# A routed expert layer: the down product of 64-row blocks with high and low rows side by side

## The chip, the cores and the metric

The kernel runs on one core of a Trainium2 chip. The metric is the device time of one execution in microseconds. All operands are float32; a product of two such matrices is made from rounded "high" parts and remainders, "low" parts, so that one float32 product costs three products on TensorE (high by high, low by high, high by low).

## The reference, cut to what matters

The layer has a mixing part (convolution, pooling, projections), a mixture of experts and a gated per-token embedding. The change touches only the mixture of experts. Each of 1024 tokens goes to 8 of 64 experts, and an expert is a SwiGLU product:

```python
def expert_block(acc, blk):
    tok, g, e = blk
    xb = xt[tok]
    hb = jax.nn.silu(xb @ w_e_gate[e]) * (xb @ w_e_up[e])
    yb = (hb @ w_e_down[e]) * g[:, None].astype(xb.dtype)
    return acc.at[tok].add(yb), None
```

D is 1024 and the hidden width FF is 256, so `hb` is 256 wide and `yb` 1024 wide. The last product, `hb @ w_e_down[e]`, is the down product.

## The kernel before, in words

The mixing part and the router take the first 770 us or so. A table in SBUF then lists the tokens of each block. The first block of an expert has up to 128 rows; further blocks, where an expert has more tokens, have up to 64 (LESS). With these inputs there are 64 first blocks, 33 further ones, and no expert has more than one further block. After them comes a closing part (embedding, gate product, final norm).

The expert stage is one loop, `Fori(0, E // 2)`, with two experts in its body (`s` is 0 or 1), written separately for each engine, with semaphores between them. Each engine first reads the plan of its expert into registers (`plan_of`, line 558: a load and then an operation and an assertion for each value): `b` the block's number, `more` the number of blocks, `behind` how many further blocks came before, `ahead` the block to gather next. `wait_at` (lines 61 to 66) is a semaphore wait on a computed value followed by an increment of a gate semaphore.

TensorE, for expert e: transposes the next expert's gathered rows (`flip_rows`, line 1086, 8 transposes), runs the first half of the gate and up product (`up`, lines 1109 to 1114), transposes the hidden rows of the block before (`flip_hidden`, line 1104), runs the second half, transposes the 64 rows of the further block if there is one (`flip_less`, line 1091), and then makes the down product of the block before, `down(b, 1 - s)` (lines 1126 to 1140, 12 products of 128x512). The down product therefore lags one block. With a further block there follow `flip_hidden`, `up_less` (lines 1097 and 1098, 16 products, with the high and low rows of 64 tokens side by side as 128 columns of weights) and a second `down`, that of the expert's own first block. So the down product of a further block is the first one of the next expert's turn, and `down` has three waits ahead of its first product (`dn_split`, `h_rounded`, `y_read`) and one, `h_split`, after four.

ScalarE rounds to the high parts: the transposed rows (`round_rows`, line 1428), two pieces of down weights (line 1461), the hidden rows (`round_hidden`, line 1444), four pieces of gate and up weights (line 1457); it makes the SiLU (line 1449) and copies the down product out of PSUM (`read_y`, line 1453). Its order within a turn is the order of the code: rows, down weights, hidden, two pieces, SiLU, two pieces, `read_y`.

VectorE makes the low parts: gate values (lines 1831 and 1832), rows (`split_rows`, line 1834), hidden (`split_hidden`, line 1855, `h_split`), two pieces of gate and up weights (line 1866), the product of gate and up (`hide`, line 1860), two more pieces, two pieces of down weights (line 1871, `dn_split`). With a further block: `split_less` (line 1842) after `hide`, and at the end `split_hidden` again, `fold` (line 1846) and `hide_less` (line 1850).

GpSimd issues the gathers of rows (line 813, into `xg`, the third buffer for further blocks) and the scatters that add a block's result to its rows in memory (line 821), in one order: gather for a later expert, gather for the next further block, scatter of the block before; with a further block of its own, a gather (if the next expert has one) and a second scatter. A scatter waits for `y_read`. SyncE issues the loads of the weights.

Lines on which the steps of the prediction rest:

```python
wait_at(pe, h_rounded, b + 1, g)
wait_at(pe, y_read, b + 1, g)
...
    if h == 0:
        wait_at(pe, h_split, b + 2, g)
```

Of the kernel before, what the change touches and what calls it, by code (L numbers as in the profile page):

```python
# [28 lines left out]
P = 128  # L29
D = 1024  # L30
# [98 lines left out]
def build(nc, i, out):  # L129
# [25 lines left out]
    plan = m.at("plan", CONST + 4 * KB, [P, EX * 4], I32).rearrange("p (e x) -> p e x", x=4)  # L155
# [300 lines left out]

    xg = [m.at("xg0", XG0, [P, D + GATES], F32)] + [room(f"xg{q}", D + GATES) for q in (1, 2)]
# [6 lines left out]
    G_P = [slots[1][:, 0:2 * FF], slots[1][:, 2 * FF:4 * FF], slots[3][:, 2 * FF:4 * FF]]  # L464
    LAST = E
# [28 lines left out]
    with ExitStack() as c:  # L494
# [44 lines left out]
        lows_kept, folded = sem("lows_kept"), sem("folded")  # L539
# [27 lines left out]
        def _(sp):  # L567
# [65 lines left out]
            sp.dma_start(g_row[:], i["g_final"]).then_inc(wp_in, 16)  # L633
# [36 lines left out]
            for load in (load_acc1, load_acc0):  # L670
                for n in range(2):
                    load(n)
            for n in range(2, NT):
# [18 lines left out]
        def _(pool):  # L692
# [183 lines left out]
            b, _, behind, _ = plan_of(pool, LAST)  # L876
# [11 lines left out]
        def _(pe):  # L888
# [237 lines left out]
            def down(b, s):  # L1126
                wait_at(pe, h_rounded, b + 1, g)
                wait_at(pe, y_read, b + 1, g)
                for h in range(NH):
                    o = Y_P[:, h * HALF:(h + 1) * HALF]  # L1130
                    for f in range(FF // P):
                        x, w = slice(f * P, (f + 1) * P), slice(f * D + h * HALF, f * D + (h + 1) * HALF)
                        nc.tensor.matmul(o, hth[:, x], dh[s][:, w], start=(f == 0), stop=False)  # L1133
                        nc.tensor.matmul(o, hth[:, x], dl[s][:, w], start=False, stop=False)  # L1134
                    if h == 0:
                        wait_at(pe, h_split, b + 2, g)
                    for f in range(FF // P):
                        x, w = slice(f * P, (f + 1) * P), slice(f * D + h * HALF, f * D + (h + 1) * HALF)
                        last = nc.tensor.matmul(o, htl[:, x], dh[s][:, w], start=False, stop=(f == 1))  # L1139
                last.then_inc(downed, 1)  # L1140
# [879 lines left out]
```

## Time and profile before

| what | us |
|---|---|
| median of 3 runs | 1837.35 |
| lowest and highest | 1836.59 and 1841.04 |
| the profiled execution's own time | 1840.77 |
| its span | 1839.0 |
| TensorE busy, share of the span | 1748.8, 95% |
| VectorE busy | 1301.4, 71% |
| ScalarE busy | 913.4, 50% |
| GpSimd busy | 783.0, 43% |

The mean granted TensorE clock is 0.982 of full speed. The shares are means over stages with different limits: VectorE's contains a convolution that lies before the experts. In the page's slices the DMA engines are 80 to 90% busy and more in the expert stage, from about 790 us to 1700 us. Start times in the timelines are microseconds from the span's start. A number such as x12 counts the instructions of a merged row, and a bracket such as [0.93 <-DVE dn_lo L1871] is the idle time of the engine just before, with what ended it. The names of engines are those of the profile: PE is TensorE, PEld its weight loads, DVE VectorE, ACT ScalarE, POOL GpSimd; a name that ends in q is the engine's instruction queue, which handles waits, branches and register work ahead of the engine itself.

### The profile page before, as it was taken

How to read it: one execution, taken by the hardware profiler on the slowest of the kernel's cores; microseconds unless marked ns; L12 is line 12 of the kernel's file. 1: busy time of each engine (PE TensorE's matmuls, PEld its weight loads, DVE VectorE, ACT ScalarE, POOL GpSimd, SP SyncE). 2: the span in 40 equal slices, each digit the busy share in tenths (PEclk: the TensorE clock that was granted, in tenths of full speed). 3: DMA queues.
4: the chain of work that ended last, by engine and by line, in shares of the span. 5: the costliest groups of instructions: out<-in, count | busy, mean ns of one | idle time of the engine just before them, and what ended most of it. 6: DMA issues, size and time to landing. Idle time of an engine off the chain costs nothing.

```text
span 1839.0 us, 32435 instructions
## 1 busy us (share of the span) xinstructions
PE 1748.8 (95%) x8044; PEld 1411.9 (77%) x8045; DVE 1301.4 (71%) x1485; ACT 913.4 (50%) x1104; POOL 783.0 (43%) x658
## 2 busy tenths in 40 slices
PE   7899999999999999799999999999999999999997
PEld 5788888878788778677777777777777777777786
DVE  7999999944365348777767877866676868676554
ACT  5101000135411223566666776666666767666665
POOL 3357667745565540144434444433343434343100
PEclk9999999999999999999999999999999999999999
DMA  4111111222233442599888999989889989887431
GB/s 153 52 46 46 46 57 68 91 92 103 98 137 131 137 161 76 207 322 335 262 283 258 337 307 298 317 273 330 270 261 319 305 277 340 277 274 224 151 113 71
DMA packets 118199, 363.39 MB, mean 198 GB/s; under 512 B 23696, under 2 KB 40208, under 8 KB 109968
## 3 DMA queue, kind: packets, MB, share of 16 engines
q1 hardware_dynamic: 70608, 276.58, 40.9%
q0 software_dynamic: 28608, 69.55, 16.5%
q10 hardware_dynamic: 18944, 16.78, 2.7%
q8 instruction: 21, 0.34, 0.1%
q14 instruction: 18, 0.15, 0.0%
HBM read 323.98 MB, written 76.85 MB: 218 GB/s over the span
## 4 chain that ended last, share of the span: by engine, by line
PE 59%; DMA 10%; issue 10%; ACT 6%; DVE 6%; POOLq 2%; ACTq 1%; DVEq 1%; POOL 1%; SPq 0%
PE bank L123 10%; PE bank L125 10%; PE bank L124 10%; DMA xg<-h_rows,cur 7%; PE bank L1133 4%; PE bank L1139 3%; PE bank L1134 3%; ACT gu_hi L1457 3%; DVE dn_lo L1871 2%; DMA dn_raw<-in_w_dn 2%; PE bank L1214 2%; PE bank L1213 2%; PE bank L1215 2%; PE bank L1097 2%; PE bank L1098 1%
## 5 line engine op out<-in xcount | busy, mean ns | idle before, releaser
L1866 DVE TENSOR_TENSOR gu_lo<-gu_raw,gu_hi 128x1024 fp32r<-128x1024 f32 x260 | 307.0, 1221 | 38.0 <-ACT gu_hi L1457 37.1
L821 POOL DMA_INDIRECT acc_rows<-y,cur x98 | 180.2, 1839 | 335.3 <-ACT y L1453 309.9
L123 PE MATMUL bank<-x_hi,w_hi 128*128 128x512 f32 x768 | 302.1, 393 | 7.7 <-ACTq L1283 6.3
L125 PE MATMUL bank<-x_hi,w_lo 128*128 128x512 f32 x768 | 299.6, 390 | 0.0
L124 PE MATMUL bank<-x_lo,w_hi 128*128 128x512 f32 x768 | 299.6, 390 | 0.0
L1602 DVE SCALAR_TENSOR_TENSOR bank<-a_buf,c_w_dw,bank 128x1024 f32<-128x1024 f32 x232 | 276.8, 1282 | 0.0
L1457 ACT CAST gu_hi<-gu_raw 128x1024 fp32r<-128x1024 f32 x260 | 260.3, 1054 | 0.0
L1109 PE MATMUL bank<-gu_hi,xh 128*128 128x512 f32 x512 | 206.5, 403 | 0.0
L1110 PE MATMUL bank<-gu_lo,xh 128*128 128x512 f32 x512 | 201.5, 394 | 0.0
L1114 PE MATMUL bank<-gu_hi,xl 128*128 128x512 f32 x512 | 195.6, 402 | 0.0
L813 POOL DMA_INDIRECT xg<-h_rows,cur x100 | 146.8, 1468 | 97.0 <-POOL cur L808 78.9
L1133 PE MATMUL bank<-dn_hi,hth 128*128 128x512 f32 x392 | 164.9, 421 | 17.0 <-DVE dn_lo L1871 11.7
L123 PEld LDWEIGHTS bank<-x_hi,w_hi 128*128 128x128 f32 x768 | 144.7, 188 | 39.4 <-issue 7.9
L187 POOL TENSOR_SCALAR w_hi<-w_raw 128x1024 fp32r<-128x1024 f32 x58 | 62.8, 1082 | 263.3 <-PE bank L125 251.1
L124 PEld LDWEIGHTS bank<-x_lo,w_hi 128*128 128x128 f32 x768 | 144.6, 188 | 31.1 <-issue 1.2
L125 PEld LDWEIGHTS bank<-x_hi,w_lo 128*128 128x128 f32 x768 | 144.6, 188 | 30.3
L1134 PE MATMUL bank<-dn_lo,hth 128*128 128x512 f32 x392 | 159.5, 407 | 0.0
L1871 DVE TENSOR_TENSOR dn_lo<-dn_raw,dn_hi 128x1024 fp32r<-128x1024 f32 x128 | 150.8, 1219 | 0.0
L189 POOL TENSOR_TENSOR w_lo<-w_raw,w_hi 128x1024 fp32r<-128x1024 f32 x58 | 142.4, 2455 | 4.8
L1453 ACT COPY y<-bank 128x1024 f32<-128x1024 f32 x98 | 99.6, 1017 | 78.9 <-PE bank L1139 78.9
L1461 ACT CAST dn_hi<-dn_raw 128x1024 fp32r<-128x1024 f32 x128 | 127.8, 1049 | 13.9 <-DMA dn_raw<-in_w_dn 13.9
L1139 PE MATMUL bank<-dn_hi,htl 128*128 128x512 f32 x392 | 127.1, 407 | 0.0
(313 smaller groups left out, 3244.7 us busy)
## 6 DMA issues: line engine op xcount, KB each, us to landing
gu_raw<-in_w_gu SPq DMA_DIRECT2D x256, 512.0 KB, 5.9
dn_raw<-in_w_dn SPq DMA_DIRECT2D x64, 1024.0 KB, 8.5
w_raw<-in_w_mix SPq DMA_DIRECT2D x60, 512.0 KB, 3.3
acc_t<-acc_rows SPq DMA_DIRECT2D x16, 512.0 KB, 4.6
first_x<-in_x SPq DMA_DIRECT2D x8, 512.0 KB, 8.2
ga_d<-stage ACTq DMA_DIRECT2D x8, 512.0 KB, 2.6
gb_d<-stage ACTq DMA_DIRECT2D x8, 512.0 KB, 2.6
gb_in<-gb_d SPq DMA_DIRECT2D x8, 512.0 KB, 3.8
```

Source lines behind the costliest of these rows:

```text
L123: nc.tensor.matmul(o, wh[:, cols], x_hi[:, k, t], start=(i == 0), stop=False)
L124: nc.tensor.matmul(o, wh[:, cols], x_lo[:, k, t], start=False, stop=False)
L125: last = nc.tensor.matmul(o, wl[:, cols], x_hi[:, k, t], start=False, stop=(i == len(ks) - 1))
L1109: nc.tensor.matmul(G_P[q], xh[q][:, x], gh[s][:, w], start=(k == 0), stop=False)
L1110: return nc.tensor.matmul(G_P[q], xh[q][:, x], gl[s][:, w], start=False, stop=(k == KC - 1))
L1114: nc.tensor.matmul(G_P[q], xl[q][:, x], gh[s][:, w], start=False, stop=False)
L1133: nc.tensor.matmul(o, hth[:, x], dh[s][:, w], start=(f == 0), stop=False)
L1134: nc.tensor.matmul(o, hth[:, x], dl[s][:, w], start=False, stop=False)
L1457: nc.scalar.copy(gh[s][:, w], rg[s][:, w]).then_inc(gu_rounded, 1)
L1602: nc.vector.scalar_tensor_tensor(out=dst, in0=src, scalar=w, in1=slots[2 + s], op0=ALU.mult, op1=ALU.add).then_inc(tap, 1)
L1866: nc.vector.tensor_tensor(gl[s][:, w], rg[s][:, w], gh[s][:, w], ALU.subtract).then_inc(gu_split, 1)
L1871: nc.vector.tensor_tensor(dl[s][:, w], rd[s][:, w], dh[s][:, w], ALU.subtract).then_inc(dn_split, 1)
```

## The change

For a 64-row block the hidden rows' high parts (64 columns) and low parts (64 columns) lie side by side in one 128-column operand. The down product then needs the down weights' high and low parts only, eight products in place of twelve; rows 0 to 63 of the result belong to the high rows and 64 to 127 to the low rows. ScalarE copies the lower half to SBUF (`y_under`), and VectorE adds the upper half to it (`fold_y`), which now releases `y_read` for such a block. VectorE's fold stands after the two pieces of down weights and ahead of the second `split_hidden`. The plan gets a fifth value, `more_last`, the number of blocks of the expert before, which each engine reads. In `down` the products are issued by kind of term: high by high, then (128-row blocks only, under a branch) low by high, then high by low; the waits for `dn_rounded`, `h_split` and `y_read` stand ahead of the first product, that for `dn_split` ahead of the third kind. Apart from that the load of `g_row` moves to the closing part, the plan table moves in SBUF, and GpSimd zeroes `y[1]` once.

```diff
+    y_under = m.at("y_under", CONST + 6 * KB, [P, D], F32)
+    hth_both = hth.rearrange("p (f c) -> p f c", f=FF // P)
+    H_L = H_T.rearrange("p (f c) -> p f c", f=FF // P)
...
@@ GpSimd @@
+            nc.gpsimd.memset(y[1][:], 0.0).then_inc(emptied, 1)
+            pool.wait_ge(emptied, 6)
             nc.gpsimd.memset(hid[:], 0.0).then_inc(hidden, 1)
...
-                    b, more, behind, ahead = plan_of(pool, e)
+                    b, more, behind, ahead, _ = plan_of(pool, e)
...
@@ TensorE @@
-            def down(b, s):
-                wait_at(pe, h_rounded, b + 1, g)
+            def down(b, s, weights, rows_64):
+                def term(x, w, start, stop):
+                    for h in range(NH):
+                        o = Y_P[:, h * HALF:(h + 1) * HALF]
+                        for f in range(FF // P):
+                            mm = nc.tensor.matmul(o, x[:, f * P:(f + 1) * P], w[:, f * D + h * HALF:f * D + (h + 1) * HALF],
+                                                  start=start and f == 0, stop=stop and f == FF // P - 1)
+                    return mm
+
+                wait_at(pe, dn_rounded, weights, g)
+                wait_at(pe, h_split, b + 2, g)
                 wait_at(pe, y_read, b + 1, g)
-                for h in range(NH):
-                    o = Y_P[:, h * HALF:(h + 1) * HALF]
-                    for f in range(FF // P):
...
+                term(hth, dh[s], True, False)
+                with pe.If(rows_64 <= 1):
+                    term(htl, dh[s], False, False)
+                wait_at(pe, dn_split, weights, g)
+                term(hth, dl[s], False, True).then_inc(downed, 1)
...
-                    wait_at(pe, dn_split, e * 2 + 2, g)
-                    down(b, 1 - s)
+                    down(b, 1 - s, e * 2 + 2, more_last)
...
-                            wait_at(pe, dn_split, e * 2 + 4, g)
-                            down(bj, s)
+                            down(bj, s, e * 2 + 4, j)
...
@@ ScalarE @@
-            def read_y(q, b):
+            def read_y(q, b, rows_64):
                 wait_at(act, downed, b + 1, g)
-                nc.scalar.copy(y[q][:], Y_P).then_inc(y_read, 1)
+                with act.If(rows_64 <= 1):
+                    nc.scalar.copy(y[q][:], Y_P).then_inc(y_read, 1)
+                with act.If(rows_64 > 1):
+                    nc.scalar.copy(y_under[0:LESS, :], Y_P[LESS:P, :]).then_inc(y_lows, 1)
...
@@ VectorE @@
-            def split_hidden(b):
+            def split_hidden(b, rows_64):
                 wait_at(dve, h_rounded, b + 1, g)
-                nc.vector.tensor_tensor(htl[:], H_T, hth[:], ALU.subtract).then_inc(h_split, 1)
+                with dve.If(rows_64 <= 1):
+                    nc.vector.tensor_tensor(htl[:], H_T, hth[:], ALU.subtract).then_inc(h_split, 1)
+                with dve.If(rows_64 > 1):
+                    nc.vector.tensor_tensor(hth_both[:, :, LESS:P], H_L[:, :, 0:LESS], hth_both[:, :, 0:LESS], ALU.subtract
+                                            ).then_inc(h_split, 1)
+
+            def fold_y(q, n):
+                wait_at(dve, y_lows, n, g)
+                nc.vector.tensor_tensor(y[q][0:LESS, :], Y_P[0:LESS, :], y_under[0:LESS, :], ALU.add).then_inc(y_read, 1)
...
                     for p in range(DOWN // PIECE):
                         split_down(s, p, e * 2 + (p + 1))
+                    with dve.If(more_last > 1):
+                        fold_y(s, behind)
                     with dve.If(more > 1):
                         with dve.Fori(1, more) as j:
                             bj = further(b, j)
-                            split_hidden(bj)
+                            split_hidden(bj, j)
                             fold(behind + j)
                             hide_less(bj)
                             with dve.If(j < more - 1):
                                 split_less(bj + 1, e)
+                            with dve.If(j > 1):
+                                fold_y(2, further(behind, j - 1))
...
```

## Rows read from the trace of the kernel before

**Rows 1.** Windows view: us; PE, PEld, DVE, ACT, POOL busy; clock; DMA share; GB/s
```profile
802.90:1694.50 891.60, 845.45 (x4070) 679.29 (x4069) 644.24 (x874) 613.80 (x780) 359.89 (x376) 0.98 0.91 292
```

**Rows 2.** The groups view of the expert stage: count, busy us and mean ns, idle before
```profile
L1453 ACT COPY y<-bank 128x1024 f32<-128x1024 f32 x97 | 98.6, 1017 | 77.1 <-PE bank L1139 77.1
...
L1834 DVE TENSOR_TENSOR xl<-bank,xh 128x1024 fp32r<-128x1024 f32 x64 | 77.9, 1217 | 33.5 <-ACT xh L1428 33.5
...
L1428 ACT CAST xh<-bank 128x1024 fp32r<-128x1024 f32 x64 | 65.1, 1017 | 53.7 <-issue 40.4 <-PE bank L1086 13.3
...
L1846 DVE TENSOR_TENSOR g_sum<-bank,low_sum 64x512 f32<-64x512 f32 x33 | 22.5, 683 | 28.7 <-ACT low_sum L1436 28.5
```

**Rows 3.** The row transposes in that stage: count, duration, first and last start
```profile
L1086 PE MATMUL bank<-ident,xg x520: 270/272/449, 779.2 to 1695.2; 128*128 128x128 f32 x174
```

**Rows 4.** TensorE's timeline, a turn without a further block, then one with
```profile
1093.63 0.39 PE L1133 MATMUL bank<-dn_hi,hth 128*128 128x512 f32 x1
...
1096.36 1.03 PE L1086 MATMUL bank<-ident,xg 128*128 128x128 f32 x8
...
1103.67 0.50 PE L1133 MATMUL bank<-dn_hi,hth 128*128 128x512 f32 x1
...
1111.76 0.47 PE L1133 MATMUL bank<-dn_hi,hth 128*128 128x512 f32 x1 [0.93 <-DVE dn_lo L1871]
...
1114.70 0.52 PE L1086 MATMUL bank<-ident,xg 128*128 128x128 f32 x3
```

**Rows 5.** VectorE's timeline in the same two turns
```profile
1092.27 0.42 DVE L1855 TENSOR_TENSOR htl<-bank,hth 128x256 fp32r<-128x256 f32 x1 [0.94 <-ACT hth L1444]
...
1098.19 2.35 DVE L1871 TENSOR_TENSOR dn_lo<-dn_raw,dn_hi 128x1024 fp32r<-128x1024 f32 x2
...
1100.59 1.21 DVE L1834 TENSOR_TENSOR xl<-bank,xh 128x1024 fp32r<-128x1024 f32 x1
1101.96 0.42 DVE L1855 TENSOR_TENSOR htl<-bank,hth 128x256 fp32r<-128x256 f32 x1 [0.16 <-ACT hth L1444]
...
1108.96 2.35 DVE L1871 TENSOR_TENSOR dn_lo<-dn_raw,dn_hi 128x1024 fp32r<-128x1024 f32 x2
1111.24 0.42 DVE L1855 TENSOR_TENSOR htl<-bank,hth 128x256 fp32r<-128x256 f32 x1
```

**Rows 6.** TensorE's instruction queue by line, 1092.9 to 1096.4
```profile
L558 PEldq SEQ_ASSERT  x4: 18/18/18, 1094.4 to 1095.3; - x4
```

**Rows 7.** That queue's semaphore events, from 1092.6 to 1092.9, then from 1092.1 to 1096.1
```profile
L66 PEldq EVENT_SEMAPHORE  x1: 51/51/51, 1092.7 to 1092.7; - x1
...
L66 PEldq EVENT_SEMAPHORE  x6: 51/51/51, 1092.2 to 1095.9; - x6
```

**Rows 8.** The branch behind the first down product, from 906 to 1189
```profile
L1167 PEldq COMPARE_BRANCH  x21: 67/77/217, 906.7 to 1188.8; - x21
```

**Rows 9.** VectorE's timeline, an expert with a further block right behind another
```profile
959.18 2.35 DVE L1871 TENSOR_TENSOR dn_lo<-dn_raw,dn_hi 128x1024 fp32r<-128x1024 f32 x2
961.45 0.42 DVE L1855 TENSOR_TENSOR htl<-bank,hth 128x256 fp32r<-128x256 f32 x1
```

**Rows 10.** TensorE's timeline in the same turn
```profile
961.98 0.47 PE L1133 MATMUL bank<-dn_hi,hth 128*128 128x512 f32 x1 [0.71 <-DVE dn_lo L1871]
...
965.57 0.63 PE L1086 MATMUL bank<-ident,xg 128*128 128x128 f32 x4 [0.59 <-issue]
```

**Rows 11.** GpSimd's timeline: a scatter and the gather for the next further block
```profile
1393.33 1.63 POOL L821 DMA_INDIRECT acc_rows<-y,cur  x1 [0.95 <-POOL cur L818]
...
1400.20 1.51 POOL L813 DMA_INDIRECT xg<-h_rows,cur  x1 [0.90 <-POOL cur L808]
```

**Rows 12.** TensorE's timeline: the transposes that wait for this gather
```profile
1408.43 0.68 PE L1091 MATMUL bank<-ident,xg 64*128 64x64 f32 x8 [2.04 <-DMA xg<-h_rows,cur]
```

**Rows 13.** The 64-row transposes of the stage: what ended the wait (us, times)
```profile
  DMA xg<-h_rows,cur: 26.6, 19
```

**Rows 14.** Windows view behind another such wait, columns as in Rows 1
```profile
1047.80:1051.20 3.40, 3.40 (x15) 2.70 (x14) 3.25 (x6) 3.31 (x5) 0.00 (x0) 0.50 1.04 327
```

More of the change, by code:

```diff
@@ L152, in build @@
     assert off[0] <= CONST + RUN
-    plan = m.at("plan", CONST + 4 * KB, [P, EX * 4], I32).rearrange("p (e x) -> p e x", x=4)
+    plan = m.at("plan", CONST + RUN, [P, EX * 5], I32).rearrange("p (e x) -> p e x", x=5)
     x_hi = m.at("x_hi", X_HI, [P, KC, S], F32R)
@@ L632, in _ @@
             sp.wait_ge(table_made, 1)
-            sp.dma_start(g_row[:], i["g_final"]).then_inc(wp_in, 16)
             for n in range(NT):
@@ L672, in _ @@
                     load(n)
+            sp.dma_start(g_row[:], i["g_final"]).then_inc(wp_in, 16)
             for n in range(2, NT):
@@ L875, in _ @@
                             scatter(1 - s, 2, bj)
-            b, _, behind, _ = plan_of(pool, LAST)
+            b, _, behind, _, _ = plan_of(pool, LAST)
             pool.wait_ge(scattered[0], 16 * (E // 2 + 1))
@@ L1151, in _ @@
                     e = r * 2 + s
-                    b, more, behind, _ = plan_of(pe, e)
+                    b, more, behind, _, more_last = plan_of(pe, e)
                     wait_at(pe, gathered[1 - s], (r + (1 + s)) * 16, g)
@@ L1216, in gate_product @@
                     last.then_inc(gate_done, 1)
-            b = plan_of(pe, LAST)[0]
+            b, _, _, _, more_last = plan_of(pe, LAST)
             flip_hidden(b)
@@ L1222, in _ @@
             embed(0)
-            pe.wait_ge(dn_split, 2 * E + 2)
-            down(b, 1)
+            down(b, 1, 2 * E + 2, more_last)
             for n in range(1, KC - 1):
@@ L1463, in _ @@
             act.sem_inc(y_read, 1)
+            act.sem_inc(dn_rounded, 2)
             for p in range(PIECES):
@@ L1474, in _ @@
                     e = r * 2 + s
-                    b, more, behind, _ = plan_of(act, e)
+                    b, more, behind, _, more_last = plan_of(act, e)
                     def round_next(ps):
@@ L1492, in _ @@
                     wait_at(act, scattered[s], r * 16 + 16, g)
-                    read_y(s, b)
+                    read_y(s, b, more_last)
                     with act.If(more > 1):
@@ L1503, in _ @@
                             wait_at(act, scattered[2], (behind + j) * 16, g)
-                            read_y(2, bj)
+                            read_y(2, bj, j)
             def round_gate(k):
@@ L1553, in _ @@
             act.wait_ge(scattered[0], 16 * (E // 2 + 1))
-            read_y(0, b)
+            read_y(0, b, more_last)
             for n in range(1, 7):
@@ L1808, in _ @@
             step(v.tensor_copy(plan[:, :, 1], blocks_f[:]))
+            step(v.memset(plan[:, 0:1, 4], 1))
+            step(v.tensor_copy(plan[:, 1:EX, 4], blocks_f[:, 0:EX - 1]))
             step(v.tensor_copy(plan[:, :, 0], cum[:]))
@@ L1869, in split_down @@
                 w = slice(p * PIECE, (p + 1) * PIECE)
-                wait_at(dve, dn_rounded, count, g)
+                wait_at(dve, dn_rounded, count + 2, g)
                 nc.vector.tensor_tensor(dl[s][:, w], rd[s][:, w], dh[s][:, w], ALU.subtract).then_inc(dn_split, 1)
@@ L1884, in _ @@
                     e = r * 2 + s
-                    b, more, behind, _ = plan_of(dve, e)
+                    b, more, behind, _, more_last = plan_of(dve, e)
                     split_rows(1 - s, b, e + 1)
-                    split_hidden(b)
+                    split_hidden(b, more_last)
                     for p in range(2):
@@ L1904, in _ @@
                                 split_less(bj + 1, e)
-            split_hidden(plan_of(dve, LAST)[0])
+                            with dve.If(j > 1):
+                                fold_y(2, further(behind, j - 1))
+            b, _, behind, _, more_last = plan_of(dve, LAST)
+            split_hidden(b, more_last)
+            with dve.If(more_last > 1):
+                fold_y(0, behind)
             def split_gate(k):
@@ L1937, in finish @@
             def finish(n):
+                if n == 0:
+                    dve.wait_ge(wp_in, 16 * (G + 3))
                 dve.wait_ge(rooted2, n + 1)
```

14 lines of the change are left out of this document (2 added, 12 removed).

## The prediction

> **What bounds the kernel now.** I read the page's slices first, then the groups of the expert stage, and then, turn by turn, the timelines of TensorE, VectorE, ScalarE and GpSimd and the row of TensorE's instruction queue. A turn is here what lies between the first row transposes of two experts, 64 of them, 520 transposes by eights with the one ahead of the loop [rows 3]. In the windows over 63 of them TensorE is busy 845 of 892 us, against 644 for VectorE and 614 for ScalarE, with DMA at 0.91 of its time [rows 1]. So TensorE looks like the bound, and four products less should be worth their time. The timelines say how near the others are. A short turn (no further block) takes 9.3 to 9.4 us, for instance from 1086.98 to 1096.36 [rows 4], without a gap on TensorE. A long turn (with a further block) takes 17.5 to 20.6, for instance 18.3 from 1096.36 to 1114.70, and TensorE waits in it: 0.9 us for dn_lo ahead of the second down product [rows 4], or for the gather of the 64 rows, 19 times, 26.6 us [rows 13]. Going by the starts of the transposes, 33 of the 64 turns are long; 13 of them follow a long turn, 12 follow a single short one and 8 follow two or more short ones or open the stage. Of the 31 short turns, 20 follow a long one, 7 are the second of their run and 4 a later one.
>
> **What goes.** The down product of a further block stands in the next turn. Products there start 0.228 us apart: 12 of them fill the 2.73 us from 1093.63 to 1096.36 [rows 4]. Four less are 0.91 us, and 33 times that is 30 us. This is the whole gain on TensorE, and it counts only where TensorE has nothing else to wait for.
>
> **What VectorE gets.** The fold is a sum of 64x1024 out of PSUM. Such a sum over 64x512 takes 683 ns, and a subtraction out of PSUM over 128x1024 takes 1217 [rows 2]; I take 1.2 us for the fold, by the row with its column count, with 1.0 and 1.4 as ends. The low part of a further block falls from 256 to 128 columns: 0.42 [rows 5] to about 0.29. Both have their place in the turn behind the further block. ScalarE's copy stays at 1.02, as the 128-row one [rows 2], since its columns don't change, and is over before VectorE comes to the fold. The fold stands between dn_lo and what VectorE does next, and there VectorE has no gap: dn_lo from 1098.19 on, xl at 1100.59, htl at 1101.96 [rows 5], and likewise dn_lo at 1108.96, htl at 1111.24. So htl comes 1.2 us later behind every fold, and `down` now waits for htl ahead of its first product, not after four.
>
> *Long turn behind a long one.* dn_lo from 959.18, htl from 961.45, over at 961.87, while TensorE starts at 961.98 and the next turn at 965.57 [rows 9, 10]. With the fold htl is over at 963.05: the first product 0.3 later (two waits are left behind it), 1.4 us later than now. The 0.91 that the first down product of the turn gives back becomes idle time in front of this wait.
>
> *Long turn behind one short turn.* The short turn's fold moves xl and htl [rows 5] by 1.2, so htl is over at 1103.55 in place of 1102.38; TensorE, which would want it 0.9 us earlier than its start at 1103.67 [rows 4], waits, and VectorE's lateness runs on through hid, dn_lo and htl to the second down product.
>
> **What TensorE's instruction queue gets.** This is the part that the busy shares hide. The queue passes the wait for htl at 1092.7, and the last semaphore event ahead of the next transposes at 1095.9 [rows 7]: 3.2 us of branch, loop edge, plan and waits, while the next transposes start at 1096.36 [rows 4]. The slack is 0.4 us. The plan's four values cost 0.3 us each (four assertions from 1094.4 to 1095.3 [rows 6]). New behind that wait are: the pair for `y_read`, 0.15 to 0.25; the branch, 0.077 when it falls through and 0.217 when it jumps [rows 8], with its compare 0.15 to 0.3; the pair for `dn_split`, 0.25; the fifth value, 0.3. Together 0.85 for a 128-row block and 1.0 for a further one. In a long turn the queue is held at the second down product, and there is no slack at all (the transposes at 965.57 waited 0.59 for issue [rows 10]): 0.85 late each time. The bounds: nothing, if the queue overlaps what the trace shows in sequence, and 1.1.
>
 The trace agrees only where no wait holds the queue; a row of 3.2 us from a passed wait to the next transposes shows that here a wait does. By the page alone the term would be nothing, and the time that of rival 1.
>
> **The sum by kinds of turn.** Each is the change of a turn's length.
> - Short behind long, 20: TensorE would be done after 8.45, the queue is ready at 5.6 (htl, 0.13 earlier) + 3.1 + 1.0, that is 9.7, against 9.35. +0.35, in all +7. The gain is not only lost but turned round.
> - Second short, 7: htl over at 16.3 (13.6 for dn_lo, 1.2, 1.2, 0.35) less 9.7 = 6.6 after the transposes, the queue ready 3.95 later, 10.5 against 9.3. +1.2, in all +8. Later ones, 4: +0.2, in all +1.
> - Long behind one short, 12: htl late by 0.6, carried to the second down product, and the queue's 0.85 + 0.2 of the later first product. +1.65, less where the gather has TensorE late anyway: 1.5, in all +18.
> - Long behind two or more short or at the start, 8: +1.1 for four. For the other four the gather decides. The scatter of a further block waits for the fold instead of ScalarE, 4.1 us later in the turn, 3 us later against the next turn's transposes, and the gather for the further block is issued behind it (1393.33, then 1400.20, awaited until 1408.43 [rows 11, 12]). +3. In all 4 + 12 = +16.
> - Long behind long, 13: +1.2 of fold and 0.8 of queue, 2.0 for ten and 1.1 for the three in which TensorE is late by the gather: +23.
>
> Sum: 7 + 8 + 1 + 18 + 16 + 23 = 73 us. ScalarE's queue gets the fifth value and two branches between read_y and the rows' rounding, about 0.5 us where it already waits 40 us in all for issue [rows 2]; I count nothing, because xl waits for VectorE's own queue of work there [rows 5], with 0.3 us in each of 31 short turns, 9 us, as the other end. The zeroing of y[1] and the plan's two further steps lie beside waits of VectorE and TensorE: at most 1 us. The later load of g_row has the whole first gate product in front of its use: nothing.
>
> **The clock.** After a wait of TensorE for a gather the granted clock fell to 0.50 for 3.4 us [rows 14], with 15 products in it. Half clock through such a stretch costs half of it, 1.7 us, of which some 0.8 lies beside the queue's new lateness and 0.9 is left. It fell in 8 of 13 waits of 1.3 to 2.7 us. In the 13 long-behind-long turns the idle stretch grows from 0.9 to 3.2 us. I take 8 us for this, between 0 and 20. The Trainium skill (same page, "HAM oscillation — how this bites in real kernels") warns of exactly this, idle stretches between bursts that put the clock back; it would raise the estimate towards the upper end.
>
> Total: +81 us. Against the profiled execution's own 1840.8 (span 1839.0) that is 1922; the median of the runs, 1837.35, is 3.4 lower, so I predict 1918.
>
> **The rivals.**
> 1. *The queue's work is hidden*, and only VectorE's fold and the gathers count. Short behind long gives 0.91 back (−18); second short +1.6 (+11); long behind one short +1.5 (+18, with the fold hitting an earlier TensorE); long behind long +1.4 for ten (+14); gathers +12. Sum +37 less 1: 1873. For it: waits in the queue are in part passed ahead of time. Against: 3.2 us in sequence.
> 2. *The gain as a count of products.* VectorE is idle a quarter of the stage (644 of 892 us); if it takes the folds in there, and the late htl falls into slack, the 132 products go: −30, 1807. It needs the fold to end before htl is wanted, and the timelines have VectorE without a gap at just that place. It decides if the fold costs less than 0.3 us.
> 3. *A cascade.* Late scatters delay gathers by a whole turn, and each wait costs the clock too: 13 + 12 turns with 2 us more. +130: 1968.
> That the change does not do what it says is hardly possible: a further block has eight products by the code.
>
> **Chances.** The forecast 0.52; rival 1 0.25; rival 2, and anything else that ends faster, 0.10; rival 3 0.10; no change 0.03. The forecast's own range is 1890 to 1950; the unknown prices (queue 0 to 1.1, clock 0 to 20, fold 1.0 to 1.4) and rival 1 take the lower end to 1848, the clock and part of rival 3 the upper to 1958. Faster by over 0.3% (5.5 us, about what a measurement of this kernel can tell): 0.10. Within it: 0.03. Slower: 0.87.
>
> **What would show it.** Right: short turns behind long ones at 9.6 to 9.9 with an idle stretch for issue ahead of the transposes; second short ones over 10; long behind long near 20 with over 2 us of idle time in front of the second down product, ended by htl; the fold at 1.2 us right behind dn_lo; scatters of further blocks 4 us later. Wrong: short turns of 8.5 us (the queue was no bound), or long turns that keep 18 us (VectorE had room), or a wait for the gather that grows in all long turns (rival 3).

## The result, and the profile after

The changed kernel takes 1983.28 us, median of 4 runs (1967.53 to 1988.81); before took 1837.37. The ratio is 1.079, 95% interval 1.077 to 1.081. The sign was forecast, the size was not: +146 us where +81 was predicted, outside the range (1848 to 1958). The profiled execution is the slowest of the four, 1988.81 with a span of 1987.1.

The windows view over the turns of [rows 1], columns as there (these windows hold 62 turns, not the 63 that the prediction counts in them):

```profile
804.43:1842.45 1038.02, 851.12 (x3941) 669.49 (x3941) 675.75 (x906) 617.88 (x781) 339.16 (x376) 0.95 0.82 252
```

The stretch is 146 us longer and no engine explains it by its work. TensorE is busy for 851 us, against 845 in [rows 1], though 129 products fewer are recorded. At 0.228 us apart these are 29 us, so what is left takes some 35 us more, an estimate, beside a mean granted clock that fell from 0.98 to 0.95. The rest is waiting. Groups of the stage (busy us, mean ns, idle before):

```profile
L1091 PE MATMUL bank<-ident,xg 128*128 128x128 f32 x501 | 67.3, 278 | 76.0 <-issue 70.9 <-DMA xg<-h_rows,cur 5.0
...
L811 POOL COPY cur<-table 128x1 int32 x94 | 56.9, 606 | 267.8 <-issue 267.8
...
L1873 DVE TENSOR_TENSOR y<-bank,y_under 64x1024 f32<-64x1024 f32 x32 | 38.6, 1207 | 0.0
```

The fold costs the 1.2 us that the prediction gave it. What it did not give is in the other lines: the row transposes wait 71 us for issue, that is for TensorE's own instruction queue, and GpSimd's copies of `cur` wait 268 us for theirs (87 in before). The waits of TensorE (us, times, longest), the transposes' in before, then three in after:

```profile
PE bank L1086 <- issue: 2.2, 6, 0.6
```

```profile
PE bank L1091 <- issue: 70.9, 51, 2.6
PE bank L1096 <- DMA xg<-h_rows,cur: 68.6, 22, 7.3
PE bank L1136 <- DVE htl L1866: 29.7, 15, 2.3
```

The middle one of the three answers to [rows 13]: 26.6 us before, 68.6 now. TensorE's timeline in the long turn of [rows 4] and the short one behind it:

```profile
1143.38 1.06 PE L1091 MATMUL bank<-ident,xg 128*128 128x128 f32 x8 [2.57 <-issue]
...
1153.20 0.68 PE L1096 MATMUL bank<-ident,xg 64*128 64x64 f32 x8 [1.46 <-DMA xg<-h_rows,cur]
...
1165.01 1.07 PE L1091 MATMUL bank<-ident,xg 128*128 128x128 f32 x8
...
1172.21 1.16 PE L1136 MATMUL bank<-dn_hi,hth 128*128 128x512 f32 x4 [0.40 <-DVE hth L1868]
1173.21 1.09 PE L1136 MATMUL bank<-dn_lo,hth 128*128 128x512 f32 x4
1176.01 1.06 PE L1091 MATMUL bank<-ident,xg 128*128 128x128 f32 x8 [1.71 <-issue]
```

The long turn takes 21.6 us in place of 18.3, the short one 11.0 in place of the 9.3 to 9.4 of before. The eight products start at 1172.21 and are done at 1174.30, and TensorE then stands 1.7 us until its queue is ready. The queues' register loads show why. Here are those of the plan on TensorE's queue in before, then in after (duration in ns: least, median, most):

```profile
L558 PEldq TENSOR_LOAD <-plan x64: 328/337/1156, 800.6 to 1700.8; - x64
```

```profile
L561 PEldq TENSOR_LOAD <-plan x61: 591/1238/3077, 801.2 to 1798.3; - x61
```

One load fetches the turn's row of the plan. Over the stage its mean rose from 0.41 to 1.29 us on TensorE's queue, 0.35 to 1.17 on VectorE's, 0.32 to 1.00 on ScalarE's, and 0.32 to 1.49 on GpSimd's, which makes two in a turn.

To say where the time went I sorted the 63 turns up to the last row transposes by kind, from the starts of these; the first turn is counted from the transposes ahead of the loop. The table gives each kind's total against before: forecast, changed kernel, and three of the experiments below.

| kind of turn (turns) | forecast | after | e1 | e2 | e7 |
|---|---|---|---|---|---|
| short behind long (19) | +7 | +29.5 | +13.9 | +4.5 | +1.3 |
| second short (7) | +8 | +9.4 | +5.1 | +6.5 | +1.1 |
| later short (4) | +1 | +1.1 | −1.7 | +11.3 | −1.7 |
| long behind one short (12) | +18 | +37.9 | +44.0 | −1.3 | −12.4 |
| long behind two or more, or first (8) | +16 | +35.0 | +21.3 | +47.0 | +9.8 |
| long behind long (13) | +23 | +35.6 | +14.9 | +27.3 | +0.5 |
| sum | 73 | 148.6 | 97.5 | 95.3 | −1.3 |

### The profile page after: what moved, and what is told of

It is laid out like the page before. It is cut to its first block, busy times and chain, and to the rows that moved or that the text cites. A ratio compares the mean times of both kernels' runs of the same rounds, so it can differ in the third digit from the quotient of the medians.

```text
span 1987.1 us, 33486 instructions
## 1 busy us (share of the span) xinstructions
PE 1751.9 (88%) x7912; PEld 1399.1 (70%) x7913; DVE 1332.8 (67%) x1520; ACT 917.6 (46%) x1104; POOL 763.1 (38%) x659
## 4 chain that ended last, share of the span: by engine, by line
PE 55%; issue 11%; DMA 7%; POOLq 6%; DVE 6%; ACT 5%; POOL 2%; ACTq 2%; DVEq 1%
PE bank L123 10%; PE bank L125 10%; PE bank L124 10%; PE bank L1136 9%; DMA xg<-h_rows,cur 7%; POOLq L561 6%; ACT gu_hi L1464 2%; DVE dn_lo L1889 2%; PE bank L1102 2%; PE bank L1103 2%; POOL cur L811 1%; PE bank L1220 1%; PE bank L1219 1%; PE bank L1218 1%; PE bank L1096 1%
## 5 line engine op out<-in xcount | busy, mean ns | idle before, releaser
L824 POOL DMA_INDIRECT acc_rows<-y,cur x98 | 159.6, 1629 | 350.8 <-ACT y L1458 174.0
L811 POOL COPY cur<-table 128x1 int32 (+1 forms) x100 | 59.9, 599 | 312.3 <-issue 280.9
L1136 PE MATMUL bank<-dn_hi,hth 128*128 128x512 f32 x392 | 123.2, 440 | 34.4 <-DVE htl L1866 30.0
L816 POOL DMA_INDIRECT xg<-h_rows,cur x100 | 116.7, 1167 | 92.9 <-POOL cur L811 66.2
L1091 PE MATMUL bank<-ident,xg 128*128 128x128 f32 x520 | 71.0, 281 | 81.3 <-issue 70.9
L1091 PEld LDWEIGHTS bank<-ident,xg 128*128 128x128 f32 x520 | 57.9, 143 | 104.9 <-issue 101.2
```

The lines of the kernel that those rows point to most:

```text
L824: nc.gpsimd.indirect_dma_start(acc_d[a], bass.IndirectOffsetOnAxis(ap=cur[3 + q][:], axis=0), y[q][:], None, bounds_check=S - 1, oob_is_er ...
L1136: mm = nc.tensor.matmul(o, x[:, f * P:(f + 1) * P], w[:, f * D + h * HALF:f * D + (h + 1) * HALF], start=start and f == 0, stop=stop and f ...
```

## The experiments

The kernel before was timed beside each; a ratio is to its runs on the same chip. Where versions were timed on different chips, the ratios are the safer comparison.

### The plan's row (e1, e2, e5, e6)

**e1**: the kernel before, with nothing but the fifth value and the plan's new place.

```diff
-    plan = m.at("plan", CONST + 4 * KB, [P, EX * 4], I32)...x=4)
+    plan = m.at("plan", CONST + RUN, [P, EX * 5], I32)...x=5)
-                    b, more, behind, _ = plan_of(pe, e)
+                    b, more, behind, _, _ = plan_of(pe, e)
```

> The kernel before with nothing but the plan's fifth value: rows of five values at the new place, loaded by every engine and used by none. Theory A (the plan's rows): the traces show the plan's load at 0.33 us before and at 0.6 us in every fourth turn and 1.2 us in the others after, on all queues, twice a turn on GpSimd; if this goes with the five-value rows alone it is there in this kernel too. TensorE's queue then is 0.9 + 0.3 later in each turn, less 0.4 of slack in the short ones: +0.8 in 31 short turns and +1.2 in 33 long ones, +65 us, 1890 to 1915. Theory B (the load is slow because the folds and the late scatters crowd the memory): loads stay near 0.35 us, and only 0.3 us for the fifth value in the long turns is left, +10 us, 1845 to 1850.

Measured: 1934.80, ratio 1.053 (1.051 to 1.055), +98 us. A value that nobody reads costs two thirds of the loss. That is 20 us above the range of theory A, and theory B (1845 to 1850) is out.

**e2**: the changed kernel with two tables of four values, one for GpSimd and one for the others.

> The changed kernel with rows of four values: the other engines read more_last in the fourth place, GpSimd has a second table with the block to gather next there. Theory A: loads back at 0.33 us; the time falls by what the fifth value costs, 65 us or more, to about 1900 to 1925, which is what the fold, the order of the terms and the late scatters cost by themselves. Theory B: loads stay slow or the waits for gathers take their place, 1960 or more.

Measured: 1935.81, ratio 1.054 (1.052 to 1.056). The loads are back at 0.33 us, and 99 us of loss are left without them. Theory A had 1900 to 1925, so more is left than it foresaw. 98 and 99 are together more than 146: both make the same things late and overlap.

**e5**: e1's rows 20 bytes apart, four values loaded. **e6**: the changed kernel with rows 32 bytes apart, five loaded (another table was moved to make room).

```diff
-                plan[0:1, bass.ds(e, 1), :].rearrange(...)     # e1
+                plan[0:1, bass.ds(e, 1), 0:4].rearrange(...)   # e5
-    plan = m.at("plan", CONST + RUN, [P, EX * 5], I32)...x=5)  # after
+    plan = m.at("plan", CONST + RUN, [P, EX * 8], I32)...x=8)  # e6, with 0:5 loaded
```

> The kernel before, with rows of the plan 20 bytes apart as in the changed kernel, of which each queue still loads the first four values; the fifth stands there and nobody reads it. Theory A (where a row starts makes the load slow: in three turns of four it starts off a 16-byte border): a load takes 0.33 us in every fourth turn and about 1 us in the others, mean 0.8 to 1.1 us, and the time is 1890 to 1935 us against 1837 before. Theory B (a fifth value to load makes it slow, wherever the row starts): loads of 0.33 us throughout and 1837 to 1845 us.

> The changed kernel with rows 32 bytes apart, all five values loaded by every queue (the table of row lists moved to make room). Theory A (where a row starts): every load takes the 0.60 us that it took in every fourth turn, and the time lies between the changed kernel's 1983 and the 1936 of the two tables of four values, nearer the second: 1940 to 1955 us. Theory B (the count of values alone): loads stay at 1.2 us and the time at 1975 to 1990 us.

Measured: e5 1894.83, ratio 1.030 (1.026 to 1.033); e6 1950.67, ratio 1.062 (1.060 to 1.065), against 1.079 for the changed kernel. TensorE's loads in e5, then in e6:

```profile
L558 PEldq TENSOR_LOAD <-plan x64: 334/1002/1848, 802.4 to 1758.7; - x64
```

```profile
L561 PEldq TENSOR_LOAD <-plan x63: 587/592/1713, 802.8 to 1798.9; - x63
```

### What is left without the loads (e3, e4, e7, e8)

**e3**: before with its twelve products by kind of term and the waits placed as in after.

> The kernel before with the twelve products issued by kind of term, for every block: waits for dn_rounded, h_split and y_read first, dn_split ahead of the third kind; no eight products, no fold, no fifth value. Theory A (the low hidden rows are wanted earlier, and one wait more stands in TensorE's queue): second down product of long turns 0.3 us later, +0.25 in the queue, +8 to +20 us in all. Rival: the third kind no longer holds up the start for dn_lo, so the 0.9 us that 23 long turns wait there goes: -10 to -20 us.

Measured: 1840.55, ratio 1.001 (1.000 to 1.003). The order of issue is nearly free; both expectations, +8 to +20 and −10 to −20 us, failed. The wait for dn_lo has become one for htl (28 us in place of 12).

**e4**: e2, with VectorE's fold, and the htl of a long turn, ahead of the down weights' low parts.

```diff
+                    with dve.If(more_last > 1):
+                        fold_y(s, behind)
+                    with dve.If(more > 1):
+                        split_hidden(further(b, 1), 1)
                     for p in range(DOWN // PIECE):
                         split_down(s, p, e * 2 + (p + 1))
-                    with dve.If(more_last > 1):
-                        fold_y(s, behind)
...
```

> As e2, and VectorE folds and makes the second low hidden rows ahead of the two pieces of down weights, not behind them. Theory A (VectorE's order decides: the fold stands in front of the low hidden rows for which TensorE waits): htl of the long turns is over about 1 us before TensorE wants it, the 2.2 us wait ahead of the second down product goes in 13 long-behind-long turns and 0.9 in the others, and the scatter of a further block is released 2.4 us earlier: 40 to 60 us less than e2, 1850 to 1880. Rival (TensorE's queue or the gathers decide): within 10 us of e2.

Measured: 1883.16, ratio 1.025 (1.023 to 1.026), 3 us above theory A's range: 53 us of the 99 were the place of the fold and of htl, which moved together. Of the rest, 36 stood in the eight turns of the table's row "long behind two or more, or first" (198.7 us for 162.7), where TensorE waited up to 9.1 us at a time for gathered rows.

**e7**: e2 without the fold; ScalarE copies the upper half to y and the lower half is left out.

> The two tables of four values (1936 us) with the eight products, but without the add on VectorE: ScalarE copies the upper half of the further block's result to y, and the lower half is left out of the output. Theory A (what is left of the loss is the fold: 1.2 us on a VectorE that has no room in a short turn, the scatter that waits for it, and the gathers behind that scatter): 1800 to 1840 us, the long waits for gathered rows gone, the scatter's instruction back at 1.6 to 2.5 us. Theory B (it is the branches and waits of the new down product in TensorE's queue): 1880 to 1930 us.

Measured: 1840.35, ratio 1.002 (1.000 to 1.004). Everything beyond the loads is the fold and what waits for it. But 1840 is the upper end of theory A: with 132 products gone, no fold and cheap loads, nothing is won. TensorE waits 76 us in the 63 turns where it waited 46 in before; the first three of its waits:

```profile
PE bank L1138 <- DVE htl L1869: 32.6, 35, 2.6
PE bank L1093 <- issue: 20.4, 31, 1.3
PE bank L1098 <- DMA xg<-h_rows,cur: 15.5, 10, 5.9
```

Of the second line 15.1 us lie in the 19 short turns behind a long one, where before has none. Four products less are worth 17.3 us there, and these turns come out at 9.40 us against 9.33: TensorE's own queue eats the gain.

**e8**: e4, with the eight products only where the turn's own expert or the next one has a further block; elsewhere twelve and ScalarE's copy.

```diff
-            step(v.tensor_copy(plan[:, 1:EX, 3], blocks_f[:, 0:EX - 1]))
+            step(v.tensor_tensor(count[:, mid], blocks_f[:, mid], blocks_f[:, 2:EX], ALU.max))
+            step(v.tensor_scalar(count[:, mid], count[:, mid], 1.0, None, ALU.min))
+            step(v.tensor_tensor(count[:, mid], count[:, mid], blocks_f[:, 0:EX - 2], ALU.mult))
...
```

> The version with the fold ahead of the split of the down weights (1883 us), with eight products only where the turn's own expert or the next one has a further block; a further block that is followed by two short experts keeps twelve products and ScalarE's copy (about 7 of 33). Theory A (the 46 us that were left come from short turns in a row, in which VectorE never pauses and GpSimd's copies and DMA instructions stand still until it does): short turns in a row and the long turn behind them return to the times of the kernel before (-40 to -55 us), so 1825 to 1843 us. Theory B (they come from each fold's own time, wherever it stands): 7/33 of 46 us back, 1868 to 1880 us.

Measured: 1832.61, ratio 0.998 (0.996 to 1.000). Some 7 folds less, 51 us less: theory A, not each fold's own time.

### GpSimd shut out (e9 to e12)

Why a fold in a short turn costs 7 us shows where GpSimd's timeline is laid beside VectorE's. From e4, a short turn behind a short one, GpSimd first:

```profile
1596.94 6.85 POOL L813 COPY cur<-table 128x1 int32 x1 [0.49 <-issue]
1604.71 1.09 POOL L818 DMA_INDIRECT xg<-h_rows,cur  x1 [0.92 <-DVE gate L1845]
```

```profile
1596.46 2.35 DVE L1887 TENSOR_TENSOR gu_lo<-gu_raw,gu_hi 128x1024 fp32r<-128x1024 f32 x2
1598.73 0.48 DVE L1881 SCALAR_TENSOR_TENSOR hid<-bank,gate,sgm 128x256 f32<-128x256 f32 x1
1599.12 2.35 DVE L1887 TENSOR_TENSOR gu_lo<-gu_raw,gu_hi 128x1024 fp32r<-128x1024 f32 x2
1601.39 2.35 DVE L1892 TENSOR_TENSOR dn_lo<-dn_raw,dn_hi 128x1024 fp32r<-128x1024 f32 x2
1603.66 0.15 DVE L1844 COPY gate<-xg 128x1 f32<-128x1 f32 x1
```

A copy of one column, 0.18 us elsewhere, takes 6.85. It starts 0.5 us after VectorE's first gu_lo and ends at 1603.79, when the chain of gu_lo, hid and dn_lo is through and the one-column copies of gate run; VectorE's next pause comes only at 1605.00. The gather behind the copy is 7 us late. In e2 it hits the scatter's instruction, 1.6 us elsewhere (twelve of them take 4.5 us, seven over 9):

```profile
1039.92 9.42 POOL L826 DMA_INDIRECT acc_rows<-y,cur  x1 [5.34 <-DVE y L1876]
```

```profile
1047.89 1.22 DVE L1847 TENSOR_TENSOR xl<-bank,xh 128x1024 fp32r<-128x1024 f32 x1
1049.38 0.42 DVE L1869 TENSOR_TENSOR htl<-bank,hth 128x256 fp32r<-128x256 f32 x1 [0.27 <-ACT hth L1450]
```

It ends at 1049.34, 0.23 us into VectorE's first pause since the scatter began; the seven scatters of over 9 us all end 0.22 to 0.24 into such a pause. The Trainium skill (SBUF — State Buffer, "Who interferes with whom") says that a VectorE instruction with two SBUF inputs contends with a GpSimd instruction that reads SBUF; the trace agrees. Of the modes in which VectorE takes both shared ports the page says that the engine that issued first has them for its whole instruction, and it reports a probe in which a tensor_tensor did not stall DMA. Here the loser waits out a whole row of instructions, hid among them, and the indirect DMA's instruction waits too. The measurement decides.

**e10, e11, e12**: in e2, in e4 and in before, the 384 subtractions (gu_lo as below, dn_lo likewise) are memsets of the same 128x1024; the low halves of the weights are left out.

```diff
-                nc.vector.tensor_tensor(gl[s][:, w], rg[s][:, w], gh[s][:, w], ALU.subtract).then_inc(gu_split, 1)
+                nc.vector.memset(gl[s][:, w].bitcast(F32), 0.0).then_inc(gu_split, 1)
```

> The two tables of four values (1936 us), where VectorE's 384 subtractions gu_lo and dn_lo (two operands read from SBUF) are memsets to zero of the same 128 x 1024 (nothing read); the low halves of the weights are left out of the result, every wait stays. Theory A (GpSimd's copies and DMA instructions stand still as long as VectorE goes from one instruction with two SBUF operands to the next): the scatter's instruction takes 1.6 us everywhere instead of up to 9.4, no copy of cur over 0.3 us, the late gathers go, and the time falls by 45 to 75 us to 1860 to 1890 us, if a memset takes the 1.22 us of the subtraction. Theory B (GpSimd's instruction is long because the DMA queue is full of other transfers): the scatter stays at 4.5 and 9.4 us and the time at 1925 to 1940 us.

> The same edit in the version with the fold ahead of the split of the down weights (1883 us). Theory A: copies of cur at 0.2 us (6.9 us before at the worst), the 10 us waits for gathered rows in the long turns behind two short ones gone, 1825 to 1850 us. Theory B (what is late is VectorE's own work, 1.2 us of fold per short turn): 1865 to 1885 us.

> The same edit in the kernel before (1837 us), as the control: what the edit is worth where no fold fills VectorE's pauses. Theory A: GpSimd's instructions fall from up to 2.7 us to 1.1 and 1.6 us, short turns stay at 9.31 us, a few of the waits of 1 to 2 us for gathered rows in long turns go: 1815 to 1837 us. Theory B: nothing on GpSimd changes and the time is 1833 to 1841 us.

Measured: 1873.58 (1.022, 1.019 to 1.025), 1829.37 (0.997, 0.995 to 0.999) and 1815.60 (0.991, 0.988 to 0.994). GpSimd's rows in e4, then in e11:

```profile
L813 POOL COPY cur<-table x89: 177/194/7338, 782.5 to 1653.6; 128x1 int32 x88, 128x1 int32<-128x1 int32 x1
L818 POOL DMA_INDIRECT xg<-h_rows,cur x89: 1022/1077/4928, 783.6 to 1655.4; - x89
```

```profile
L813 POOL COPY cur<-table x95: 179/185/763, 780.6 to 1653.7; 128x1 int32 x94, 128x1 int32<-128x1 int32 x1
L818 POOL DMA_INDIRECT xg<-h_rows,cur x95: 1025/1066/1093, 781.7 to 1654.9; - x95
```

All three lie in theory A's ranges. No instruction of GpSimd is long any more, in all three (copies take 0.77 us at most, a scatter 2.35). So the subtractions hold GpSimd up, and not a full DMA queue. Which property of theirs does it, the runs don't separate. A memset takes 0.91 us and the next starts 1.074 us after it, which leaves VectorE a hole of 0.16 us; subtractions start 1.13 us apart and leave none. The memsets also give VectorE 0.3 us a turn. The difference of the edit in e4 and in before, 54 − 20 us, is what the shut-out costs e4 more.

**e9**: e4, and VectorE waits for GpSimd's copy ahead of the first gu_lo.

```diff
                     split_hidden(b, more_last)
+                    wait_at(dve, picked, e + 4, g)
```

> The version with the fold ahead of the split of the down weights (1883 us), and in each turn VectorE waits, ahead of the first gu_lo, until GpSimd has made its copy of cur for the next gather. Theory A (GpSimd is shut out by VectorE without a pause): the wait costs VectorE up to 1 us in some turns, but no copy takes 2 to 7 us any more and the gathers behind two short turns come a turn earlier: 1840 to 1875 us. Theory B (VectorE's own time): every wait adds to it, 1885 to 1910 us.

Measured: 1864.34, ratio 1.016 (1.012 to 1.021). One more wait for VectorE in every turn and the kernel is 15 us faster than e4 by the ratios, 19 by the medians: theory A. The longest copy is 1.7 us; one gather's instruction still takes 4.9.

### Where TensorE's 30 us are (e13 to e18)

e7 left this open for the long turns. Their second down product there waits for htl behind gu_lo and dn_lo. **e13** is e7, **e14** is e8, **e15** is e3 (twelve products) with another order on VectorE in long turns (the last two pieces of gu_lo behind what the turn itself needs; e13 and e15 have no fold to move):

```diff
                     with dve.If(more > 1):
                         split_less(b + 1, e)
+                        for p in range(DOWN // PIECE):
+                            split_down(s, p, e * 2 + (p + 1))
+                        with dve.If(more_last > 1):
+                            fold_y(s, b)
+                        split_hidden(further(b, 1), 1)
+                        for p in range(2, 4):
+                            split_up(1 - s, p, r * 8 + (4 * s + 5 + p))
...
```

> The version without the fold (1840 us), with VectorE's order changed in turns whose expert has a further block: the down weights' low halves and htl come ahead of the last two pieces of gu_lo, which only the next turn's products read. The lower half of the further block's result is left out, as there. Theory A (TensorE's 30 us from 132 products less are there, but in a turn with a further block the second down product starts or ends by VectorE's chain gu_lo, dn_lo, htl, so they turn into waits for it): with the chain shortened by two pieces, 2.3 us, the gain comes out: 1790 to 1820 us. Theory B (the gain is eaten by the loads of the next weights, which fill 91 per cent of the DMA engines' time already): 1830 to 1842 us.

> The version with eight products only where the turn's own expert or the next has a further block (1833 us), with the same order on VectorE: down weights' low halves, fold, htl, then the last two pieces of gu_lo. Theory A: TensorE's queue passes its last wait of a double turn some 2 us earlier, and the next row transposes come up to 1.7 us earlier in 33 turns: 1785 to 1815 us. Theory B: 1825 to 1838 us.

> The control without eight products: the kernel before with its twelve products issued by kind of term (1841 us), and the same order on VectorE. It says whether the eight products are worth anything beside the order. Theory A (the order frees VectorE's chain for either; four products less are then 0.91 us less in the turns where TensorE is the bound): 1800 to 1825 us, above the version with eight by 5 to 20 us. Theory B (twelve products are as good, since the fold costs what they save): within 4 us of the version with eight.

Measured: 1834.97 (1.000, 0.998 to 1.002), 1841.21 (1.003, 1.000 to 1.005), 1850.42 (1.006, 1.004 to 1.009). Theory A failed as to the time in all three; e13 lies in theory B's range, e14 3 us above it, and e15 is 9 us slower than e14, as theory A had it and theory B had not. The mechanism worked (in e13 the wait ahead of the second down product is gone, 6.0 and 14.7 us in two kinds of long turn), but the time came back one step on.

TensorE's waits in e14 for rows of further blocks:

```profile
PE bank L1098 <- DMA xg<-h_rows,cur: 42.3, 21, 4.4
```

GpSimd issues that gather behind the scatter of the turn's first block, which waits for a product of the same turn. **e16, e17, e18** are e14, e15 and e8 with the gather first:

```diff
+                    with pool.If(more <= 1):
+                        scatter_first()
                     with pool.If(more > 1):
                         with pool.Fori(1, more) as j:
...
+                            with pool.If(j <= 1):
+                                scatter_first()
```

> The version with eight products and the low halves of the weights in the later order (1841 us), in which TensorE waited 42.3 us for rows gathered for further blocks, 28 of them where one double turn follows another. There GpSimd issues that gather behind the scatter of the turn's first block, which waits for a result still to be computed. Here the gather goes ahead of that scatter. Theory A (the time that the chain on VectorE gave back went into this one place in GpSimd's queue): the waits fall to 15 us or less and the time by 20 to 35 us, to 1805 to 1822 us. Theory B (the gather is late by the DMA engines, busy with weights): 1835 to 1845 us.

> The same edit in the control with twelve products (1850 us). If eight products are worth their fold once neither VectorE's chain nor the gather decides, this one is 5 to 20 us above the version with eight; if the fold costs what they save, within 4 us of it. In numbers: 1815 to 1838 us by theory A, 1843 to 1853 us by theory B.

> The same edit in the version with eight products where there is room and VectorE's order with the last pieces of gu_lo ahead of the down weights (1833 us). Its waits for rows of further blocks were 14 us only, so theory A gives 1820 to 1832 us, and theory B no change, 1829 to 1836 us. It says which of the two orders is better once the gather comes first.

Measured: 1819.42 (0.991, 0.988 to 0.994), 1808.69 (0.986, 0.983 to 0.989), 1835.61 (1.000, 0.998 to 1.001). e16's waits, then e17's:

```profile
PE bank L1099 <- issue: 15.4, 20, 1.4
PE bank L1104 <- DMA xg<-h_rows,cur: 10.0, 8, 2.3
PE bank L1110 <- DVE xh L1868: 9.0, 15, 0.7
```

```profile
PE bank L1097 <- DMA xg<-h_rows,cur: 20.5, 12, 4.6
...
PE bank L1092 <- issue: 2.6, 1, 2.6
```

The order on GpSimd takes 22 us off e14 and 42 off e15, and nothing off e8 (that is e18), whose VectorE has the older order: with eight products it pays only together with VectorE's order. With twelve products it was not tried alone. Theory B of e13, that the loads of the weights eat the gain, is out: e17 moves the same weights 27 us faster. e17 is the fastest of all and beats both kernels: the twelve products of before by kind of term (e3, no gain by itself), with VectorE's and GpSimd's orders changed. The version with eight where there is room (e16) is 11 us behind it. In short turns behind long ones TensorE's queue shows (13.1 us of idle time, none in e17), and in long behind long ones TensorE waits 8.3 us for xh, 1.6 in e17; how much of this is the fold's is open, since no run has this order with eight products and no fold. Both theories of e17 fell: the eight products with their fold and branches cost more than they save.

## Why the prediction was wrong

- **The step that failed is the fifth value's price.** The prediction put it at 0.3 us ("The plan's four values cost 0.3 us each", then "the fifth value, 0.3"), read off four assertions [rows 6]. The load in the same queue was not looked at: 0.9 us more in three turns of four and 0.25 in the fourth, on four engines. e1 measures the step by itself: +98 us, of which the forecast held at most 19 (0.3 us in 63 turns). The upper bound of the whole queue term, 1.1 us, was passed by this one value: 0.9 for the load and the 0.3 that was counted.
- **"I count nothing" for the other queues** failed for the same reason. The largest part of e1's loss, 44 us, lies in long turns behind a short one, where TensorE waits 42 us for gathered rows, 11 before: GpSimd's two loads, up to 3 us each, stand in its queue ahead of the gather. No run slows GpSimd's loads alone, so that share of the loss is read from the trace and not tested.
- **The rest of the sum was near as a total, in part by luck, and wrong in its parts.** Without the loads (e2) the loss is 99 us, 95 in the turns, for 73 and 8 of clock. Long behind long +27 (forecast +23) and second short +6.5 (+8) stand. Long behind one short was +18 and is −1; in e7, without the fold, it is −12, so the four products do count there. Long behind two short was +16 and is +47: the scatter is late as foreseen, but its instruction then stands still for up to 9.4 us and the gathers slip by a turn, so rival 3's cascade exists, with a cause that it did not name.
- **The queue without the loads** was forecast at +0.35 us for a short turn behind a long one, rival 1 at −0.91. e16 against e17 has 9.68 against 9.34, e2 has 9.57 and e7 9.40 against 9.33 of before, but e4, with another order on VectorE, 8.89. So this step stood: the queue's work takes the whole gain in some orders and a part in others, and the full 0.91 came back in none. The queue of 64 entries that the Trainium skill gives TensorE (TensorE: Matmul & The Clock Gate, Part 1) did not hide it.
- **The clock** was put at 8 us, between 0 and 20. In after the work left to TensorE takes about 35 us more; part of this lies beside waits, and no run separates it. Left open.
- **Rival 2**, the gain as a count of products, needed a free VectorE. e7 takes the fold off it, and there is still no gain: three more chains stand right behind TensorE's (its own queue in short turns, VectorE's htl, then GpSimd's gather in long ones). The prediction had the first two; it had the gather late only by way of the fold.

## What to carry to other kernels

Price a register load from its own rows, and keep what a queue loads per turn in four words on a 16-byte border; a value more can cost more than the instructions it saves. When an engine is filled up to where it never pauses, look at what GpSimd does in that time. Before taking work off the busiest engine, follow the chains that end with it: here three more stood right behind TensorE's, and changing the order on two other engines was worth 27 us where taking products away was worth none.

## What the runs showed of the hardware

- A TENSOR_LOAD of the plan: 0.33 us (four int32 on a 16-byte border), 0.59 (five, on it), 1.00 (four, off it), 1.24 (five, off it), on TensorE's queue, and the medians within 0.12 of these on the others. On GpSimd's queue 49 of 130 loads took over 1.5 us in after, up to 2.8, and none over 0.35 in before; why is open.
- A GpSimd copy of 128x1 took 6.85 us, and the instruction of an indirect DMA 9.42, while VectorE went from one instruction to the next without a pause. The copy ended with VectorE's row of gu_lo, hid and dn_lo, the scatters of over 9 us only in its next pause. With memsets in place of the subtractions, and holes of 0.16 us between them, none took over 0.8 and 2.4 us.
